# The first mixer's value projection as three split products instead of one of full precision

## The reference

```python
q, i, f_fw, f_bw, g = jnp.split(h @ w_in, 5, axis=-1)
...
qx, vx, (kxf, lxf), (kxb, lxb), gx = gates(hx)      # vx = heads(i): the values
ox_f, _ = gla_chunkwise(qx, kxf, vx, lxf, sc_f)
```

## Time and profile before

| | |
|---|---|
| median of 3 runs | 3349.37 us (3347.96 to 3357.53) |
| the profiled execution | 3347.44 us |
| its span, first to last instruction | 3345.6 us |
| mean granted TensorE clock | 0.949 |
| TensorE (PE) busy | 2969.4 us, 89% |
| VectorE (DVE) busy | 2146.4 us, 64% |
| ScalarE (ACT) busy | 1195.6 us, 36% |
| PE L693, split projections | 768 instructions |
| PE L700, value projection | 512 instructions |

### The profile page before, as it was taken

The page is one execution under the profiler, slowest core; times in us unless marked ns, Lnnn a source line. Parts: engine busy times, 40 slices in busy tenths (PEclk is TensorE's granted clock), DMA queues, the critical chain, the costliest instruction groups (busy, mean ns, idle before and its releaser), DMA issues.

```text
span 3345.6 us, 45434 instructions
## 1 busy us (share of the span) xinstructions
PE 2969.4 (89%) x16149; PEld 2475.1 (74%) x16149; DVE 2146.4 (64%) x4006; ACT 1195.6 (36%) x2081; POOL 513.3 (15%) x323
## 2 busy tenths in 40 slices
PE   7799987797577999999999999599717899999997
PEld 1488874571476999999999999466616799999997
DVE  0256554399794777777777777534599565666666
ACT  0222220320493333333333333123309444444443
POOL 0000000322102333333333333000510000000000
PEclk9899998898898999999999999889859999999999
DMA  6311111425368787878877877310306656566654
GB/s 260 142 60 63 63 51 51 151 79 199 115 198 287 270 280 271 281 272 281 274 278 276 277 278 247 117 44 32 128 24 176 236 209 211 204 212 213 211 209 144
DMA packets 216326, 616.86 MB, mean 184 GB/s; under 512 B 15496, under 2 KB 97584, under 8 KB 209968
## 3 DMA queue, kind: packets, MB, share of 16 engines
q1 hardware_dynamic: 179388, 481.70, 40.9%
q0 software_dynamic: 36864, 134.23, 11.9%
HBM read 567.54 MB, written 48.33 MB: 184 GB/s over the span
## 4 chain that ended last, share of the span: by engine, by line
PE 75%; DVE 15%; DMA 4%; issue 2%; ACT 2%; DVEq 1%; POOL 1%; SPq 0%; ACTq 0%; POOLq 0%
PE bank L889 27%; PE bank L900 26%; PE bank L693 5%; PE bank L788 2%; DVE arena L1550 2%; DMA arena<-in_wst 2%; PE bank L735 2%; DVE arena L1551 2%; PE bank L700 2%; PE bank L658 2%; PE bank L822 1%; DVE arena L1449 1%; DVE arena L1452 1%; DVE arena L1450 1%; PE bank L975 1%
## 5 line engine op out<-in xcount | busy, mean ns | idle before, releaser
L889 PE MATMUL bank<-h_parts,u_hi 128*128 128x384 f32 (+1 forms) x4096 | 902.5, 311 | 33.0 <-DVE u_lo L1555 33.0
L900 PE MATMUL bank<-v_parts,p_hi 128*128 128x512 f32 x2560 | 794.1, 391 | 0.4 <-DVE p_lo L1571 0.3
L889 PEld LDWEIGHTS bank<-h_parts,u_hi 128*128 128x128 f32 x4096 | 706.7, 191 | 53.7 <-issue 34.2
L889 PE MATMUL bank<-h_parts,u_lo 128*128 128x384 f32 (+1 forms) x2048 | 637.4, 311 | 0.0
L900 PEld LDWEIGHTS bank<-v_parts,p_hi 128*128 128x128 f32 x2560 | 470.8, 188 | 87.6 <-DVE p_lo L1571 1.0
L900 PE MATMUL bank<-v_parts,p_lo 128*128 128x512 f32 x1280 | 500.7, 391 | 0.0
L1567 DVE TENSOR_TENSOR arena<-arena 128x384 f32<-128x384 f32 (+1 forms) x256 | 190.7, 745 | 438.6 <-ACT arena L1190 437.9
L1190 ACT ACTIVATE arena<-bank 128x384 f32<-128x384 f32 (+1 forms) x256 | 111.7, 436 | 974.2 <-PE bank L889 974.2
L889 PEld LDWEIGHTS bank<-h_parts,u_lo 128*128 128x128 f32 x2048 | 391.6, 191 | 0.0
L1555 DVE TENSOR_TENSOR u_lo<-arena,u_hi 128x1024 fp32r<-128x1024 f32 x256 | 312.9, 1223 | 114.8 <-ACT u_hi L1183 86.1
L1569 DVE TENSOR_TENSOR v_parts<-arena,v_parts 128x1024 fp32r<-128x1024 f32 x256 | 313.7, 1225 | 45.9 <-ACT v_parts L1193 37.5
(11 more groups left out here) (216 smaller groups left out, 3629.2 us busy)
## 6 DMA issues: line engine op xcount, KB each, us to landing
arena<-in_u SPq DMA_DIRECT2D x256, 512.0 KB, 4.6
arena<-in_v SPq DMA_DIRECT2D x256, 512.0 KB, 3.6
arena<-in_wst SPq DMA_DIRECT2D x39, 2048.0 KB, 7.6
gate_scratch<-arena SPq DMA_DIRECT2D x20, 2048.0 KB, 8.7
arena<-gate_scratch SPq DMA_DIRECT2D x32, 768.0 KB, 5.0
arena<-in_whd SPq DMA_DIRECT2D x8, 2560.0 KB, 9.1
arena<-gate_scratch SPq DMA_DIRECT2D x32, 512.0 KB, 4.4
x_scratch<-arena SPq DMA_DIRECT2D x10, 512.0 KB, 3.1
```

What stands on the lines that cost most here:

```text
L889: last = mm(banks[q][:, 0:ND[p]], w[:, q, col], h[:, k, DS[p]], start=(n3 == 0), stop=(n3 == 3 * KT - 1))
L900: last = mm(banks[2 + 2 * b + half][:, :], x[:, q, b * P:(b + 1) * P], y[:, q, col], start=(first and i == 0), stop=(final and i == 2))
```

## The change

The value weights are split like the others, into the free buffers `v_parts` (`weight_parts(2 + slot)`, one pair per slot), and each piece is made of three split products per feature block with 128 tokens stationary and 128 weight columns streamed. ScalarE and VectorE make the parts at level 6 of the head before; in the opening they do it after the last sigmoid and after the last projection block's subtraction. The semaphores now count five parts per head.

```diff
-                    pe.wait_ge(hw_l, 4 * g + (c + 1))
+                    pe.wait_ge(hw_l, 5 * g + (c + 1))
...
-            def value_piece(slot, b, final):
-
+            def value_piece(g, slot, b, final):
+
+                w_hi, w_lo = weight_parts(2 + slot)
+                rows = slice(b * P, (b + 1) * P)
+                if b == 0:
+                    pe.wait_ge(hw_l, 5 * g + 5)
                 for k in range(KT):
-                    last = mm(banks[7][:, b * P:(b + 1) * P], hT[:, k, b * P:(b + 1) * P], wh(slot)[:, k, 4 * P:5 * P],
-                              start=(k == 0), stop=(k == KT - 1))
+                    for i, (x, w) in enumerate(((h_hi, w_hi), (h_hi, w_lo), (h_lo, w_hi))):
+                        last = mm(banks[7][:, rows], x[:, k, rows], w[:, k, :], start=(k == 0 and i == 0), stop=(k == KT - 1 and i == 2))
...
+            def high_v(slot):
+                af_(weight_parts(2 + slot)[0], wh(slot)[:, :, 4 * P:5 * P], ACT.Copy).then_inc(hw_h, 1)
...
                     if more and l in (2, 4):
                         high_w(1 - slot, l // 2 + 1)
+                    if more and l == 6:
+                        high_v(1 - slot)
...
                 if c < 2:
                     high_w(0, c + 2)
+            high_v(0)
             act.wait_ge(w_loaded[1], 16 * (MT + 1))
             high_w(1, 0)
             values(0, 0)
...
+            def low_v(g, slot):
+                hi, lo = weight_parts(2 + slot)
+                dve.wait_ge(hw_h, 5 * g + 5)
+                V.tensor_tensor(lo, wh(slot)[:, :, 4 * P:5 * P], hi, ALU.subtract).then_inc(hw_l, 1)
...
                     if more and l in (2, 4):
                         low_w(h + 1, 1 - slot, l // 2 + 1)
+                    if more and l == 6:
+                        low_v(h + 1, 1 - slot)
...
             for c in range(2, 4):
                 low_w(0, 0, c)
+            low_v(0, 0)
             low_w(1, 1, 0)
             scale_head(0, 0)
```

More of the change, by code:

```diff
@@ L709, in _ @@
             for b in range(NB):
-                value_piece(0, b, b == NB - 1)
+                value_piece(0, 0, b, b == NB - 1)
             def head(h, slot, more):
@@ L745, in head @@
                 if more:
-                    value_piece(1 - slot, 0, False)
+                    value_piece(h + 1, 1 - slot, 0, False)
                 for d in range(2):
@@ L756, in head @@
                     if more:
-                        value_piece(1 - slot, 1 + d, False)
+                        value_piece(h + 1, 1 - slot, 1 + d, False)
                 for b in range(NB):
@@ L770, in head @@
                 if more:
-                    value_piece(1 - slot, 3, True)
+                    value_piece(h + 1, 1 - slot, 3, True)
                 pe.wait_ge(sq_done, h + 1)
@@ L1285, in low_w @@
                 hi, lo = weight_parts(c % 2)
-                dve.wait_ge(hw_h, 4 * g + (c + 1))
+                dve.wait_ge(hw_h, 5 * g + (c + 1))
                 V.tensor_tensor(lo, wh(slot)[:, :, c * P:(c + 1) * P], hi, ALU.subtract).then_inc(hw_l, 1)
+            def low_v(g, slot):
+                hi, lo = weight_parts(2 + slot)
+                dve.wait_ge(hw_h, 5 * g + 5)
+                V.tensor_tensor(lo, wh(slot)[:, :, 4 * P:5 * P], hi, ALU.subtract).then_inc(hw_l, 1)
             for c in range(2):
```

## The result

The changed kernel takes 3419.97 us (median of 6 runs, 3396.46 to 3426.21) against 3353.45 us of the kernel before (6 runs, 3347.77 to 3370.12). The ratio is 1.0181 with a 95% interval of 1.0152 to 1.021: slower by 1.8%, where 31.7 us, 0.9%, were forecast, and above the stated range. The profiled execution took 3414.01 us, span 3412.2 us, mean granted clock 0.940.

What follows compares the result with a forecast made beforehand. The prediction took TensorE, on the chain of waits in the first mixer, as the bound. Value products +28.7 and opening gap +3.0 made +31.7 us on 3347.44, so 3379.1, stated as 3380; range 3368 to 3400.

Steps and rivals of the forecast that it cites:

- The price of a narrow split product: Value pieces: 0.112 us per 128-column product, set by its weight load; 0.90 us more per piece, +28.7 us over 32.
- rival 3: Value pieces: load and stream in series, 0.164 us a product, 3.94 us a piece, total 3421; chance 3 in 100.
- rival 1: Value pieces: narrow products stream at their own length, under 0.075 us each, totals such as 3342 or 3338; chance 8 in 100.
- rivals 2 and 3: Value pieces: split products cost 0.224 us (3467, chance 9 in 100), or load and stream in series (3421, 3 in 100).
- The four-pass rule: Value pieces: fp32 takes four passes, reduced form one; a piece would cost 1.34 us, bringing 14 us before the stall.
- 32 pieces on the chain, nothing hidden or gained: First mixer: four value pieces for each of eight heads delay the end in full; head period 49.8 us.
- ScalarE and VectorE within a head at nothing: Level 6 of a head: rounding copy (1.05 us) and subtraction (1.23 us) fit into idle time, costed at nothing.
- The gap of 3.0 us in the opening: Opening: the first value piece waits for late value parts until 161.65, TensorE standing still on the chain, +3.0 us.
- The clock in the gap: Opening: no clock loss taken after the 3 us gap because 23 dense us precede it; upper end 1.5 us.
- The clock within the heads: First mixer's heads: granted clock of 1.00, as in the rows of before; no loss in the sum.
- The direction: Whole kernel: slower by more than about 0.3% (10 us), chance 0.92; within it 0.05, faster 0.03.
- theory D: From the experiments: clock falls where TensorE waits; narrow products behind keep it down, 256-column and full-precision ones do not.

Runs made afterwards that it cites:

- e4: Changed kernel with value parts still made and waited for, but the full-precision products of before; 3360.4 us, ratio 1.0012 to the kernel before.
- e2: Changed kernel without the product of tokens' high part and weights' low part, 16 instructions per piece; 3379.71 us, ratio 1.0059 to the kernel before.
- e3: Changed kernel with each split product streaming 256 columns instead of 128 (values wrong); 3398.88 us, ratio 1.012 to the kernel before.
- e7: Changed kernel with the opening's value parts made early and half of value piece 0 ahead of the transposes; 3379.25 us, ratio 1.0065 to the kernel before.
- e10: Changed kernel, opening's value parts still late, with half of value piece 0 ahead of the transposes; 3388.71 us, ratio 1.0088 to the kernel before.

## Why the prediction was wrong

- *The price of a narrow split product: right.* 0.112 us was said, 0.110 measured at full clock (2.63/24). The one-column weight loads were the row to go by. All three rivals are out by the same number, although the total came out at rival 3's 3421; that is a coincidence, for what was added is lost clock, not a load in series. Of the two supports for the price one was weak: that the old instruction's 0.112 us is its weight load. A quarter of the 0.435 us that 512 columns take at full precision is 0.109, so its stream alone accounts for it. (The totals of rival 1, but for its 3357, are counted from 3347.4 and those of rivals 2 and 3 from 3349.4, a difference of 2 us that decides nothing.) The four-pass rule of the Trainium skill ("FP8 and Floating Point Precision", TensorE Precision Notes) would give 1.34 us a piece if a reduced product takes one pass, a count that is the prediction's reading; at 128 columns the measured 2.63 us speaks against it.
- *32 pieces on the chain, nothing hidden or gained: right.* Heads whose clock held have a period of 49.7 us, 49.8 was said.
- *ScalarE and VectorE within a head at nothing: right* (`e4`, heads of 46.2 us).
- *The gap of 3.0 us in the opening: right in its length* (2.9), also that it is on the chain.
- *The clock in the gap: the step that failed.* The prediction took 0 with 1.5 us as the upper end, on the ground that 23 dense us stand before it. The clock fell even so, in every trace with that gap. Full-precision products made up for it at 1.9 us (`e4`), the narrow ones stayed at half clock to the end of the values: 8.2 us and 1.9 behind them. The upper end was taken from a dense block of wide products and moved to a stretch of another kind.
- *The clock within the heads: not foreseen.* The prediction held 1.00 there because the rows of before showed it. In the profiled execution this was 15.4 us (one tail 9.8, three starts 4.8, head 7 0.8). What showed that the instruction's kind matters: `e2` against `e4`, as many instructions behind the same waits and slower; `e3`, twice the columns and faster than the change. What speaks for the wait beside it: `e7`, the same products without the wait and at full clock.
- *The direction* was right (slower, 0.92). The profiled execution grew by 66.6 us where 31.7 were forecast, 34.9 more. The term of the clock in the mixer is 25.5 of them (8.2 + 1.9 + 15.4), and with it alone the forecast would have left its range. Layer 1's attention is 11.8, which the change did not cause as far as the traces show; the other terms together take 2.4 off.

What stays open: why a tail falls in one head and not in the next, identical one, and why one head start was cold in `e10` without a wait before its narrow products. The runs show the falls move from trace to trace, not what picks them. For the tails theory D rests on 14 heads without the wait in two traces and on the smaller scatter of one timed kernel; for the opening it rests on six traces with the gap and six without. Why narrow split products keep the clock down, while full-precision ones of the same shape do not, no run here shows.

## What to carry to other kernels

Price a matmul by the longer of its stream and its weight load: three products of 128 columns with a load each (2.63 us for eight feature blocks) cost more than two instructions at full precision (1.79 us). And ask of narrow products not only their price but what clock they leave: behind even a short TensorE wait they can run at half clock until wide or full-precision work comes, so close the waits before them, or turn the product round so that the long side streams (24 x 512 columns plus four transposes, 0.4% faster than before, with the wait filled).

## What the runs showed of the hardware

- At a granted clock of 0.50 narrow split products take 0.209 us each (5.01/24) and 0.110 at 1.00: their pace follows the granted clock. At 1.00 it is that of the weight loads in the earlier trace rows, 0.111 us.
- TensorE at 100% busy by the page's measure ran 15.9 us at 0.50. Busy time does not say what the clock will do.
- A gap of 2.9 us behind 23 us of dense wide products was followed by a lower clock in all six traces that have it (the change twice, `e2`, `e3`, `e4`, `e10`) and in none of the six that do not. Full-precision products and those of 256 columns were back at 1.00 some 5 us on.
